# Page copies held until the fourth product, nine weight slots instead of eight, expert loops of three items

## The chip, the cores and the metric

The kernel runs on one core of a Trainium2 chip. The metric is the device time of one execution in microseconds (us). A core has TensorE (matrix products; PE in the profile), VectorE (DVE), ScalarE (ACT), GpSimd (POOL) and SyncE (SP), which here only issues transfers, and 16 DMA engines that move data between HBM and the on-chip memory. SyncE, ScalarE and GpSimd each issue into queues of their own, and a queue's transfers run on all 16 DMA engines.

## The reference

One inference step of a hybrid decoder layer over 256 prompt tokens and 64 sampled ones (8 requests of 8 tokens), all in float32:

```
u = rmsnorm(x)
z = u @ w_in + b_in                       # 1024 -> 6968 columns, feeds both mixers and both gates
h_m = mlstm(z)                            # short convolution, matrix memory
h_n = nsa(z, cache_kv[page_table], ...)   # compressed, selected and window attention
x = x + (g_m * (h_m @ w_bm) + g_n * (h_n @ w_bn)) @ w_out
v = rmsnorm(x)
for each expert e among the top 4 of 32 of a token:
    gu = v @ w_gu[e] + b_gu[e]            # 1024 -> 2048: gate and up
    x += weight * (swiglu(gu) @ w_dn[e] + b_dn[e])
y = rmsnorm(x) * normf_g
```

The past keys and values of the 8 requests lie in 64 pages of a pool, in the order of a page table. Besides `y` the step returns the new keys and values, the convolution rows and the memory states. Each expert has 8 MB of gate and up weights and 4 MB of down weights, and all 32 are read: 403 MB.

## The kernel before, in words

The work of each engine is written out by hand; engines meet at semaphores, and each engine and each issuing queue goes through its own list in order.

The front (`front`) normalises the tokens and multiplies them with `w_in`, which SyncE loads in column chunks of 2 MB into two slots (L122, in `load_chunk`). Chunks 0 and 1 give eight products with the weights held still (L382; each ends with a step of the semaphore `s_pd`); a chunk's slot is free after its four products, and SyncE then loads the chunk after the next one: the third chunk waits for `s_pd` 4, the fourth for `s_pd` 8. The third to sixth chunks give token products in four groups of three (L401, L405), each group from one chunk. Beside this, GpSimd makes constants and masks and then copies the 64 cache pages into one linear tensor in HBM, `kv_linear` (L290), each copy behind a small load of the page's number. After the copies stand, on GpSimd's list, the stores of the convolution rows and the memory states. Attention over the prompt and over the samples follows the front.

The last part (`tail`) merges the branches (L1983), multiplies with `w_out` (L1994, L2003), routes tokens to experts and runs the experts. Work comes as items: an item is up to 64 tokens of one expert, at least one item for each of the 32 experts. The weights of an item are six chunks of 2 MB (four of gate and up, two of down), each in a slot of a ring of `NSLOT` tiles. Chunk n of the whole stream goes to slot `SLOT_ORDER[n % NSLOT]`. Six of the slots are tiles of their own, which first hold the branch weights (slots 0 to 3) and `w_out` (4 and 5); the others lie in the big tile `zf`, whose earlier contents are dead by then. SyncE issues the first `NSLOT` chunks as these become free: the first four after pairs of branch products (`s_pe`), two after the gating of the branches (`s_ev`), the rest after the output projection (`s_po`). From then on chunk n waits for the use of the chunk that had its slot, counted by `s_used` (L1716, in `load_chunk_of`).

TensorE does an item in two functions: `gate_up` (L2133, one use of a chunk after each two of eight steps, with the scatter of the item before in the middle) and `down` (L2174), which first gathers and transposes the next item's tokens. Because slots must be known when the program is built, the loop over items has a body of four items (`QUADS` turns of it; 4 x 6 chunks are three rounds of eight slots), and the items after that, up to a count known only on the chip, run in a loop of one item that always uses the same six slots. Two loads of items stand ahead of the loop on SyncE. The small buffers of an item (`xe`, `atT`, `y3`, `oh`, `up`, `sg` and others) lie in the upper part of `zf`. The gain of the final norm, repeated over the partitions (`gf`, three loads), is loaded by SyncE ahead of the first expert chunk.

Of the kernel before, what the change touches and what calls it, by code (L numbers as in the profile page):

```python
# [45 lines left out]
NE = 32  # L46
FE = 1024
SLOT = 64
N_OVER = 20
NITEM = NE + N_OVER  # L50
NCHUNK = 6
NSLOT = 8
SLOT_ORDER = (0, 1, 2, 3, 6, 7, 4, 5)

# [70 lines left out]
def front(nc, m, a):  # L125
# [59 lines left out]
    with ExitStack() as c:  # L185
# [51 lines left out]
        def _(pool):  # L237
# [47 lines left out]

            pool.wait_ge(s_pages, 16)
            for b in range(NB):
                for j in range(NPG):
                    page = pool.value_load(m.pages[0:1, b * NPG + j:b * NPG + j + 1], min_val=0, max_val=a.cache_kv.shape[0] - 1)
                    pool.dma_start(m.kv_lin[b, j], a.cache_kv[bass.ds(page, 1)].rearrange("n r l c g d -> r (n l c g d)")).then_inc(s_lin, 16)  # L290
# [1417 lines left out]
def load_chunk_of(sp, m, a, e, c, slot):  # L1708

    if c < 4:  # L1710
        src = a.w_gu[0, bass.ds(e, 1), c * 256:(c + 1) * 256, :].rearrange("e (p j) n -> p (e j) n", p=128)
        dst = m.ring[slot][:, :].rearrange("p (j n) -> p j n", j=2)
    else:
        src = a.w_dn[0, bass.ds(e, 1), (c - 4) * 512:(c - 3) * 512, :].rearrange("e (p j) n -> p (e j) n", p=128)
        dst = m.ring[slot][:, :].rearrange("p (j n) -> p j n", j=4)
    sp.dma_start(dst, src).then_inc(m.s_slot[slot], 16)  # L1716


def load_gain(sp, tile, gain, sem):

    sp.dma_start(tile[:, 0:2, :].rearrange("p h n -> p (h n)"), gain.to_broadcast((128, D))).then_inc(sem, 16)
    for h in range(2):
        sp.dma_start(tile[h * 64:(h + 1) * 64, 2, :], gain[:, h * H:(h + 1) * H].to_broadcast((64, H))).then_inc(sem, 16)


def tail(nc, m, a):
# [27 lines left out]
    s_oh, s_ohe, s_gat, s_xg = sem("ex_onehot"), sem("ex_onehot_e"), sem("ex_gathered"), sem("ex_x")  # L1754
    s_xh, s_xr, s_xm, s_xl = sem("xn2_high"), sem("xn2_rest"), sem("xn2_middle"), sem("xn2_low")
    s_yh, s_yr, s_ym, s_ohz = sem("ex_y_high"), sem("ex_y_rest"), sem("ex_y_middle"), sem("ex_onehot_dup")
# [7 lines left out]
    PER = 4  # L1764
    QUADS = 7
    SCATTER_BANKS = (6, 7, 4, 5, 0)
# [5 lines left out]
    flat_zf = m.zf[:, :, :].rearrange("p k n -> p (k n)")  # L1772
    m.ring += [flat_zf[:, 0:4096], flat_zf[:, 4096:8192]]
    at_word = 8192

    def carve(n):
        nonlocal at_word
        at_word += n
        return flat_zf[:, at_word - n:at_word]

    def halves(words, parts):
        return words.bitcast(BF).rearrange("p (t s) -> p t s", t=parts)

    WORDS = PARTS * H // 2
    xT = flat_zf[:, 8192:10240].rearrange("p (k n) -> p k n", k=KD)
    xe, atT = (carve(4 * 2 * SLOT).rearrange("p (k h s) -> p k h s", k=4, h=2) for _ in range(2))
    y3 = halves(carve(3 * H // 2), 3)
    oh = carve(NT * SLOT).rearrange("p (t s) -> p t s", t=NT)
    ohe = carve(SLOT)[0:3 * NE, 0:SLOT // 2].bitcast(BF)
    assert at_word == 10240  # L1790
    xg, gt, up, sg, y_rest = (carve(H) for _ in range(5))
    xT2 = gt.rearrange("p (k n) -> p k n", k=4)
    with ExitStack() as c:
        def sb(name, shape, dt=FP):
            return c.enter_context(nc.sbuf_tensor(name, shape, dt))

        x = sb("x", [128, PARTS, H])
        xn = sb("xn2", [128, PARTS, H])
        g2, gf = sb("g2b", [128, 3, H]), sb("gf", [128, 3, H])
        g2c, br, wr = sb("g2c", [128, KD]), sb("brb", [128, NE]), sb("w_r", [128, KD, NE])  # L1800
        t1 = xn[:, 0, 0:NTOK]
        words = lambda t: t[:, :, :].rearrange("p t s -> p (t s)")
        x_rest, g2w = words(xn), words(g2)
        b_rest = x_rest[0:3 * NE, H:H + 2 * FE]
        xs_high, xs_mid = halves(m.masks[:, 0:WORDS], PARTS), halves(g2w[:, 0:WORDS], PARTS)
        xs_low = [halves(g2w[:, WORDS:WORDS + H // 2], 1), halves(x_rest[:, 0:H], 2), halves(x_rest[:, H:2 * H], 2)]
# [23 lines left out]
        sel, sel_b = sb("sel", [128, NT, NE]), sb("sel_b", [128, 2, NE], BF)  # L1830
        posT = sb("posT", [NE, NT * 128])
        cnt, ext, cse, cs = (sb(n, [NE, 1]) for n in ("cnt", "ext", "cse", "cs"))
# [5 lines left out]
        own = of_expert[0:NE, NE:NITEM]  # L1838
        bdn = sb("bdn", [SLOT + NE, H])
        wtT2 = sb("wtT", [SLOT + NE, NT * 128])  # L1840
# [11 lines left out]
        def slot_of(i, ch):  # L1852
            return SLOT_ORDER[(NCHUNK * i + ch) % NSLOT]

        def round_of(i, ch):
            return (NCHUNK * i + ch) // NSLOT

        @block.sync
        def _(sp):
# [16 lines left out]
            sp.dma_start(br[:, :], a.b_router.to_broadcast((128, NE))).then_inc(s_g, 16)  # L1876
            load_gain(sp, gf, a.normf_g.rearrange("(o n) -> o n", o=1), s_gf)
            for n in range(NSLOT):
# [7 lines left out]
            for n in range(NSLOT, 2 * NCHUNK):  # L1886
                sp.wait_ge(s_used, n + 1 - NSLOT)
                load_chunk_of(sp, m, a, 1, n - NCHUNK, slot_of(1, n - NCHUNK))
            with sp.Fori(0, QUADS) as q:
                for j in range(2, 6):  # L1890
                    for ch in range(NCHUNK):
                        sp.wait_ge(s_used, 4 * NCHUNK * q + (NCHUNK * j + ch + 1 - NSLOT))
                        load_chunk_of(sp, m, a, 4 * q + j, ch, slot_of(j, ch))
            sp.wait_ge(s_tab, 1)
            nw = n_items(sp)
            with sp.Fori(4 * QUADS + 2, nw) as i:
                e = sp.value_load(etab[0:1, bass.ds(i, 1)], min_val=0, max_val=NE - 1)

                for ch in range(NCHUNK):
                    sp.wait_ge(s_used, NCHUNK * i + (ch + 1 - NCHUNK))  # L1900
                    load_chunk_of(sp, m, a, e, ch, slot_of(1, ch))
# [15 lines left out]
        def _(pe):  # L1917
# [277 lines left out]
            nw = n_items(pe)  # L2195
            pe.wait_ge(s_xl, 1)
            down(1, first_slot, lambda ch: 16)
            with pe.Fori(0, QUADS) as q:
                for j in range(1, 5):
                    slot = lambda ch: slot_of(j, ch)  # L2200
                    loaded = lambda ch: 16 * 3 * q + 16 * (round_of(j, ch) + 1)
                    gate_up(4 * q + j, slot, loaded)
                    down(4 * q + (j + 1), slot, loaded)
            later = 4 * QUADS + 1
            slot = lambda ch: slot_of(later, ch)
# [9 lines left out]
        def _(act):  # L2215
# [52 lines left out]
            act.wait_ge(s_wtT, 1)  # L2268
            copy(posT[:, :], m.bank[0][0:NE, 0:NT * 128], s_wTe)
            act.wait_ge(s_wtT, 2)  # L2270
# [4 lines left out]
            copy(words(xs_high), x_rest, s_xh)  # L2275
            act.wait_ge(s_xr, 1)
            copy(words(xs_mid), x_rest, s_xm)
            act.wait_ge(s_own, 1)
# [39 lines left out]
        def _(dve):  # L2318
# [194 lines left out]
            dve.wait_ge(s_xh, 1)  # L2513
            dve.tensor_tensor(x_rest, x_rest, words(xs_high), ALU.subtract).then_inc(s_xr, 1)
            add_bias()
            dve.wait_ge(s_xm, 1)
            for low, r, n in zip(xs_low, (0, 1, 3), (1, 2, 2)):
# [193 lines left out]
```

## Time and profile before

| | us |
|---|---|
| median of three runs (lowest, highest) | 1600.58 (1599.12, 1600.83) |
| the profiled execution | 1597.34 |
| its span (first to last recorded work) | 1595.7 |
| TensorE busy, share of the span | 1513.4, 95% |
| VectorE busy, share | 546.0, 34% |
| ScalarE busy, share | 316.4, 20% |

The page gives each engine's busy time, the span in 40 equal slices (here 39.9 us each), the DMA queues, the chain of work that ended last, the costliest groups of instructions and the DMA issues. Times in the views count from the start of the span. A group is a line of the kernel, an engine, an operation and its operands; "idle before" is what the engine waited just before it, and the arrow names what ended that wait. In views of one row for several instructions the first number is the start of the first and the second the time to the end of the last. The granted clock of TensorE is a share of 2.4 GHz.

### The profile page before, as it was taken

Reading aid. Unit: us, or ns where it says so; the run is one execution under the profiler, and the core shown is the slowest. Engines: PE = TensorE matmul, PEld = TensorE weight load, DVE = VectorE, ACT = ScalarE, POOL = GpSimd, SP = SyncE. Lnnn points to the kernel's source line nnn. Section 1 sums busy time; section 2 is a strip of 40 time slices with the busy share of each in tenths; the row PEclk is TensorE's granted clock in tenths of the full one; section 3 lists DMA queues with packets and bytes.
Section 4 is the critical chain, followed back from the end, with each engine's and each line's share of the span. In section 5 each row is a group of like instructions: output and inputs, shape, how many; then the busy total and the mean of one; then the engine's idle time right before and its main releaser. Section 6 shows DMA issues by size and latency. Waiting matters only on the chain.

```text
span 1595.7 us, 22043 instructions
## 1 busy us (share of the span) xinstructions
PE 1513.4 (95%) x8565; PEld 712.0 (45%) x8565; DVE 546.0 (34%) x1184; ACT 316.4 (20%) x711; POOL 53.5 (3%) x121
## 2 busy tenths in 40 slices
PE   8999998999989999999999999999999999999996
PEld 5547554666766675333333333333333333333332
DVE  4511333244457432623323232232322322322323
ACT  2301221234236400311111111111111111111112
POOL 5410000000000000000000000000000000000000
PEclk9999998799999999999999999999999999999998
DMA  9933356134464396699999999999999999999995
GB/s 344 390 126 106 119 185 133 54 106 182 146 172 160 92 304 284 238 374 427 428 428 427 428 428 428 428 427 427 428 428 428 428 427 428 428 428 428 426 427 225
DMA packets 99712, 507.33 MB, mean 318 GB/s; under 512 B 19126, under 2 KB 57386, under 8 KB 73896
## 3 DMA queue, kind: packets, MB, share of 16 engines
q1 hardware_dynamic: 95522, 482.78, 76.2%
q0 software_dynamic: 4080, 23.73, 4.0%
q8 instruction: 38, 0.62, 0.2%
q14 instruction: 18, 0.15, 0.0%
q10 hardware_dynamic: 54, 0.05, 0.0%
HBM read 499.38 MB, written 28.06 MB: 331 GB/s over the span
## 4 chain that ended last, share of the span: by engine, by line
PE 32%; DMA 30%; DVE 3%; issue 1%; SPq 0%; ACT 0%; DVEq 0%
DMA wring<-w_gu 25%; PE bank L2133 14%; PE bank L2174 8%; DMA zf<-w_gu 4%; PE bank L1983 3%; PE bank L1994 2%; PE bank L2075 1%; PE bank L1966 1%; DVE zf L2504 1%; DVE zf L2506 1%; DVE zf L2502 1%; DMA wring<-w_branch_n 1%; PE bank L2003 0%; PE bank L1962 0%; PE bank L2108 0%
## 5 line engine op out<-in xcount | busy, mean ns | idle before, releaser
L2133 PE MATMUL bank<-wring,zf 128*64 128x512 f32 x1600 | 360.4, 596 | 25.0 <-DMA wring<-w_gu 24.7
L2133 PEld LDWEIGHTS bank<-wring,zf 128*64 128x64 f32 x1600 | 108.7, 136 | 250.3 <-issue 192.4
L2486 DVE SCALAR_TENSOR_TENSOR x<-bank,wt,x 128x512 f32<-128x512 f32 x155 | 104.9, 744 | 196.3 <-PE bank L2075 196.3
L2174 PE MATMUL bank<-wring,zf 128*64 128x512 f32 x768 | 170.1, 595 | 0.7
L2217 ACT ACTIVATE zf<-bank 128x512 f32<-128x512 f32 (+1 forms) x133 | 75.8, 594 | 316.1 <-PE bank L2174 214.8
L2133 PE MATMUL bank<-zf 128*64 128x512 f32 x448 | 100.8, 596 | 6.2 <-DMA zf<-w_gu 6.2
L2492 DVE TENSOR_TENSOR zf<-bank,zf 128x512 f32<-128x512 f32 x32 | 22.1, 692 | 224.6 <-ACT zf L2217 224.6
L2174 PEld LDWEIGHTS bank<-wring,zf 128*64 128x64 f32 x768 | 53.4, 137 | 98.9 <-issue 96.9
L954 PE MATMUL bank<-uT,w_slots 128*128 128x320 f32 x256 | 81.1, 465 | 1.2 <-ACT zf L1087 1.2
L2075 PE MATMUL bank<-zf,eqw 64*128 64x512 bf16 x558 | 69.3, 380 | 0.0
L1983 PE MATMUL bank<-zf,wring 128*128 128x320 f32 x240 | 65.1, 433 | 1.6 <-DMA wring<-w_branch_n 1.3
L2217 ACT ACTIVATE eqw<-bank 128x320 bf16<-128x320 f32 x32 | 14.0, 438 | 259.4 <-PE bank L2075 259.4
L2133 PEld LDWEIGHTS bank<-zf 128*64 128x64 f32 x448 | 31.2, 136 | 68.7 <-issue 54.9
L2499 DVE TENSOR_SCALAR zf<-bank 128x512 f32<-128x512 f32 x32 | 22.1, 692 | 112.8 <-PE bank L2133 112.6
L954 PEld LDWEIGHTS bank<-uT,w_slots 128*128 128x128 f32 x256 | 49.7, 204 | 22.7 <-issue 5.8
L2284 ACT ACTIVATE zf<-zf 128x512 f32<-128x512 f32 x32 | 20.1, 629 | 192.3 <-DVEq L2500 192.3
L2174 PE MATMUL bank<-zf 128*64 128x512 f32 x256 | 56.7, 595 | 0.0
L1983 PEld LDWEIGHTS bank<-zf,wring 128*128 128x128 f32 x240 | 45.4, 190 | 21.3 <-DMA wring<-w_branch_n 1.8
L401 PE MATMUL bank<-w_slots,uT 128*128 128x512 f32 (+1 forms) x128 | 52.1, 566 | 2.4 <-DMA w_slots<-w_in 2.4
L2075 PEld LDWEIGHTS bank<-zf,eqw 64*128 64x128 bf16 x558 | 23.3, 98 | 56.3 <-issue 38.3
L1966 PE MATMUL bank<-ident,zf 128*128 128x128 f32 x260 | 35.9, 280 | 11.6 <-DVEq L2507 11.3
L2102 PE MATMUL bank<-g2b,eqw 128*64 128x512 bf16 (+1 forms) x224 | 44.3, 385 | 0.0
(530 smaller groups left out, 1699.3 us busy)
## 6 DMA issues: line engine op xcount, KB each, us to landing
wring<-w_gu SPq DMA_DIRECT2D x100, 2048.0 KB, 32.6
wring<-w_dn SPq DMA_DIRECT2D x48, 2048.0 KB, 34.5
zf<-w_gu SPq DMA_DIRECT2D x28, 2048.0 KB, 32.8
zf<-w_dn SPq DMA_DIRECT2D x16, 2048.0 KB, 34.3
w_slots<-w_in SPq DMA_DIRECT2D x11, 2048.0 KB, 8.7
kv_linear<-cache_kv POOLq DMA_DIRECT2D x64, 256.0 KB, 5.3
kv_stage<-kv_linear SPq DMA_DIRECT2D x16, 1024.0 KB, 9.2
w_slots<-w_in SPq DMA_DIRECT2D x4, 1024.0 KB, 7.8
```

The lines of the kernel that those rows point to most:

```text
L401: last = pe.matmul(m.bank[n % 4][:, 0:width], uT[:, k, t * 128:(t + 1) * 128], w[:, s, k, 0:width], start=(k == 0), stop=(k == KD - 1))
L954: last = pe.matmul(m.bank[7][:, 0:NTOK], m.w_slots[:, chunk % NSL, k, j % 4 * 128:(j % 4 + 1) * 128], m.uT[:, k, :], start=(k == 0), stop= ...
L1966: last = pe.transpose(m.bank[bank][:, k * 128:(k + 1) * 128], src[:, k * 128:(k + 1) * 128], m.ident[:, :])
L1983: last = pe.matmul(m.bank[2 * i + f % 2][:, 0:NTOK], wb[:, i, k, f % 2 * 128:(f % 2 + 1) * 128], h[:, k, :], start=(k == 0), stop=(k == KD ...
L1994: last = pe.matmul(m.bank[4 + 2 * t + h][:, :], mT[:, k, t * 128:(t + 1) * 128], w_out(k, h), start=(k == 0), stop=(k == KD - 1))
L2075: last = pe.matmul(out, ohtb[rows, t * 128:t * 128 + TILE_ROWS[t]], y3[rows, q, :], start=(q == 0), stop=(q == 2))
L2102: last = pe.matmul(half(0, h), oh2[rows, t, 0:SLOT], x_part(q, 2 * t + h if t < 2 else 4)[rows, :], start=(t == 0 and q == 0), stop=(t == ...
L2133: last = pe.matmul(half(2 + gu, h), xe[:, k % 4, k // 4, :], m.ring[slot(k // 2)][:, o:o + H], start=False, stop=(k == KD - 1))
L2174: last = pe.matmul(half(4, h), atT[:, k % 4, k // 4, :], m.ring[slot(4 + k // 4)][:, o:o + H], start=(k == 0), stop=(k == 7))
L2217: act.activation(dst, src, ACT.Copy).then_inc(to, 1)
L2486: dve.scalar_tensor_tensor(part(r), m.bank[SCATTER_BANKS[r]][:, :], wt[:, r // 2, bass.ds(i - 1, 1)], part(r), ALU.mult, ALU.add).then_inc ...
L2492: dve.tensor_tensor(y_rest, m.bank[4][:, :], y3[:, 0, :], ALU.subtract).then_inc(s_yr, 1)
```

## The change

Three edits are made together.

1. GpSimd waits for the fourth product (`s_pd` 4) before the first page copy.
2. The ring has nine slots. The ninth is the part of `zf` where the item's buffers lay. These buffers move into a tile of their own (`item_work`, `item_x`) and into tiles that are dead by then (`xn2`, `bdn`, the tile of the transposed logits). The final gain has no tile any more: it is loaded into slot 3 of the ring, which the last items do not use, after its last chunk was used. Two pairs of semaphores become one each, with two counts.
3. The loops have a body of three items and nine turns (3 x 6 chunks are two rounds of nine slots), so the loop of one item starts at item 28 for TensorE (29 before) and at load 29 for SyncE (30 before).

```diff
-NSLOT = 8
-SLOT_ORDER = (0, 1, 2, 3, 6, 7, 4, 5)
+NSLOT = 9
+SLOT_ORDER = (0, 1, 2, 3, 6, 7, 4, 5, 8)
...
             pool.wait_ge(s_pages, 16)
+            pool.wait_ge(s_pd, 4)
             for b in range(NB):
...
-    QUADS = 7
+    TRIPLES = 9
...
-    m.ring += [flat_zf[:, 0:4096], flat_zf[:, 4096:8192]]
+    m.ring += [flat_zf[:, 0:4096], flat_zf[:, 4096:8192], flat_zf[:, 8192:12288]]
...
-    xg, gt, up, sg, y_rest = (carve(H) for _ in range(5))
+    gt = flat_zf[:, 12288:12288 + H]
...
-        g2, gf = sb("g2b", [128, 3, H]), sb("gf", [128, 3, H])
+        g2, work = sb("g2b", [128, 3, H]), sb("item_work", [128, 3 * H])
+        gf = m.ring[3][:, 0:3 * H].rearrange("p (h n) -> p h n", h=3)
+        xe, y3 = by_half(work[:, 0:H]), halves(work[:, H:H + 3 * H // 2], 3)
...
+        xg = sb("item_x", [128, H])[:, :]
...
+        up, sg, y_rest = (x_rest[:, (2 + i) * H:(3 + i) * H] for i in range(3))
...
-        bdn = sb("bdn", [SLOT + NE, H])
+        bdn_words = sb("bdn", [128, H])
+        bdn, atT = bdn_words[0:SLOT + NE, :], by_half(bdn_words[:, :])
...
-            load_gain(sp, gf, a.normf_g.rearrange("(o n) -> o n", o=1), s_gf)
             for n in range(NSLOT):
...
-            with sp.Fori(0, QUADS) as q:
-                for j in range(2, 6):
+            with sp.Fori(0, TRIPLES) as q:
+                for j in range(2, 5):
                     for ch in range(NCHUNK):
-                        sp.wait_ge(s_used, 4 * NCHUNK * q + (NCHUNK * j + ch + 1 - NSLOT))
-                        load_chunk_of(sp, m, a, 4 * q + j, ch, slot_of(j, ch))
+                        sp.wait_ge(s_used, 3 * NCHUNK * q + (NCHUNK * j + ch + 1 - NSLOT))
+                        load_chunk_of(sp, m, a, 3 * q + j, ch, slot_of(j, ch))
+            sp.wait_ge(s_used, NCHUNK * 3 * TRIPLES + 4)
+            load_gain(sp, gf, a.normf_g.rearrange("(o n) -> o n", o=1), s_gf)
             sp.wait_ge(s_tab, 1)
             nw = n_items(sp)
-            with sp.Fori(4 * QUADS + 2, nw) as i:
+            with sp.Fori(3 * TRIPLES + 2, nw) as i:
...
-            with pe.Fori(0, QUADS) as q:
-                for j in range(1, 5):
+            with pe.Fori(0, TRIPLES) as q:
+                for j in range(1, 4):
```

On GpSimd, at the first page copy after the masks, the list reads before as follows (the semaphore `s_pages` is `pages_in`, `s_pd` is `mx_done`):

```order
L247 AFFINE_SELECT seq_onehot<-seq_onehot 64x8
L289 TENSOR_LOAD pages [waits pages_in]
L289 ISA x2
L290 ISA
L290 DMA kv_linear<-cache_kv 16x4096
```

and with the change:

```order
L247 AFFINE_SELECT seq_onehot<-seq_onehot 64x8
L290 TENSOR_LOAD pages [waits mx_done,pages_in]
L290 ISA x2
L291 ISA
L291 DMA kv_linear<-cache_kv 16x4096
```

Nothing changes its place there; the first load of a page number has a second wait, and the 64 copies and all that follows stand behind it.

On SyncE, where the last part's loads end and the expert chunks begin, the list before (`wring` 0 to 5 are slots 0 to 5, `zf` the slots behind them):

```order
L1876 DMA brb<-b_router 128x32
L1721 DMA gf<-normf_g 128x1024
L1723 DMA gf<-normf_g 64x512 x2
L1716 DMA wring0<-w_gu 128x4096
L1716 DMA wring1<-w_gu 128x4096
L1716 DMA wring2<-w_gu 128x4096
L1716 DMA wring3<-w_gu 128x4096
L1716 DMA zf<-w_dn 128x4096 x2
L1716 DMA wring4<-w_gu 128x4096
L1716 DMA wring5<-w_gu 128x4096
L1716 DMA wring0<-w_gu 128x4096
L1716 DMA wring1<-w_gu 128x4096
```

and with the change, from the second chunk on:

```order
L1717 DMA wring1<-w_gu 128x4096
L1717 DMA wring2<-w_gu 128x4096
L1717 DMA wring3<-w_gu 128x4096
L1717 DMA zf<-w_dn 128x4096 x2
L1717 DMA wring4<-w_gu 128x4096
L1717 DMA wring5<-w_gu 128x4096
L1717 DMA zf<-w_gu 128x4096
L1717 DMA wring0<-w_gu 128x4096
L1717 DMA wring1<-w_dn 128x4096
L1717 DMA wring2<-w_dn 128x4096
```

The three loads of `gf` are gone from this place, and a chunk into `zf` stands before the first chunk that waits for a use. Behind the loop over three items the list on SyncE now has:

```order
L1887 COMPARE_AND_BRANCH
L1722 DMA wring3<-normf_g 128x1024
L1724 DMA wring3<-normf_g 64x512 x2
L1846 TENSOR_LOAD etab
L1846 ISA x2
L1896 UNCONDITIONAL_BRANCH
```

The loads of the gain stand between the two loops, ahead of the load of the item count (`etab`).

## Rows read from the trace of the kernel before

**Rows 1.** The page's second part: clock and traffic in 40 slices of 39.9 us.
```profile
PEclk9999998799999999999999999999999999999998
...
GB/s 344 390 126 106 119 185 133 54 106 182 146 172 160 92 304 284 238 374 427 428 428 427 428 428 428 428 427 427 428 428 428 428 427 428 428 428 428 426 427 225
```

**Rows 2.** The chain in order of time: start us, us, what.
```profile
719.85 6.87 PE bank L2133 x32
...
938.72 6.87 PE bank L2133 x32
...
1030.11 35.35 DMA wring<-w_gu
...
1118.36 35.34 DMA wring<-w_gu
...
1565.65 3.68 PE bank L2133 x16
```

**Rows 3.** TensorE's timeline, 60 to 105: start us, us, line, operation [idle before].
```profile
63.85 15.70 PE L401 MATMUL bank<-w_slots,uT 128*128 128x512 f32 x32 [2.38 <-DMA w_slots<-w_in]
...
83.97 13.90 PE L401 MATMUL bank<-w_slots,uT 128*128 128x512 f32 x32
...
101.41 14.00 PE L401 MATMUL bank<-w_slots,uT 128*128 128x512 f32 x32
```

**Rows 4.** Windows of 1 us: busy by engine, granted clock, DMA share, GB/s.
```profile
62.00:63.00 1.00, 0.00 (x0) 0.00 (x0) 0.87 (x1) 0.59 (x3) 0.21 (x1) 1.00 0.99 375
66.00:67.00 1.00, 1.00 (x2) 0.34 (x1) 0.06 (x2) 0.98 (x2) 0.49 (x1) 0.50 1.12 442
```

**Rows 5.** Windows over the start of the weight stream, columns as in rows 4.
```profile
590.00:596.00 6.00, 6.00 (x24) 4.21 (x23) 3.43 (x4) 0.00 (x0) 0.00 (x0) 1.00 1.08 324
626.00:649.00 23.00, 22.75 (x115) 9.46 (x113) 8.55 (x32) 3.37 (x10) 0.00 (x0) 1.00 0.01 2
651.40:686.20 34.80, 33.28 (x195) 14.02 (x195) 21.06 (x57) 13.54 (x19) 0.00 (x0) 0.95 0.88 354
686.20:690.20 4.00, 4.00 (x22) 1.31 (x20) 0.00 (x0) 0.00 (x0) 0.00 (x0) 1.00 0.26 53
691.00:985.00 294.00, 289.71 (x1584) 104.88 (x1581) 91.79 (x162) 42.66 (x75) 0.00 (x0) 1.00 1.01 427
```

**Rows 6.** SyncE's timeline, 640 to 700: expert chunks issued.
```profile
649.33 18.55 SPq L1716 DMA_DIRECT2D wring<-w_gu  x4
674.06 3.76 SPq L1716 DMA_DIRECT2D wring<-w_dn  x2
688.85 3.75 SPq L1716 DMA_DIRECT2D zf<-w_gu  x2
```

**Rows 7.** GpSimd's timeline: the first and the last of 64 page copies.
```profile
12.52 0.72 POOL L290 DMA_DIRECT2D kv_linear<-cache_kv  x1 [0.68 <-issue]
...
84.01 0.49 POOL L290 DMA_DIRECT2D kv_linear<-cache_kv  x1 [0.63 <-issue]
```

**Rows 8.** Line 122 alone: loads of w_in, issue (duration, start) and landing.
```profile
L122 SPq DMA_DIRECT2D w_slots<-w_in x1: 2313/2313/2313, 39.9 to 39.9; - x1
...
DMA to landing us min/median/max: 23.9/23.9/23.9
...
L122 SPq DMA_DIRECT2D w_slots<-w_in x1: 367/367/367, 57.1 to 57.1; - x1
...
DMA to landing us min/median/max: 19.6/19.6/19.6
...
L122 SPq DMA_DIRECT2D w_slots<-w_in x1: 367/367/367, 83.2 to 83.2; - x1
...
DMA to landing us min/median/max: 13.3/13.3/13.3
```

**Rows 9.** DMA issues of the final gain: count, KB each, median us to landing.
```profile
gf<-normf_g SPq DMA_DIRECT2D x1, 512.0 KB, 14.3
...
gf<-normf_g SPq DMA_DIRECT2D x2, 128.0 KB, 14.5
```

More of the change, by code:

```diff
@@ L1754, in tail @@
     s_oh, s_ohe, s_gat, s_xg = sem("ex_onehot"), sem("ex_onehot_e"), sem("ex_gathered"), sem("ex_x")
-    s_xh, s_xr, s_xm, s_xl = sem("xn2_high"), sem("xn2_rest"), sem("xn2_middle"), sem("xn2_low")
+    s_xh, s_xl = sem("xn2_high_then_middle"), sem("xn2_rest_then_low")
     s_yh, s_yr, s_ym, s_ohz = sem("ex_y_high"), sem("ex_y_rest"), sem("ex_y_middle"), sem("ex_onehot_dup")
@@ L1772, in tail @@
     flat_zf = m.zf[:, :, :].rearrange("p k n -> p (k n)")
-    m.ring += [flat_zf[:, 0:4096], flat_zf[:, 4096:8192]]
[L1774 to L1779, printed above, removed]
+    m.ring += [flat_zf[:, 0:4096], flat_zf[:, 4096:8192], flat_zf[:, 8192:12288]]
     def halves(words, parts):
@@ L1785, in tail @@
     xT = flat_zf[:, 8192:10240].rearrange("p (k n) -> p k n", k=KD)
[L1786 to L1790, printed above, removed]
-    xg, gt, up, sg, y_rest = (carve(H) for _ in range(5))
+    gt = flat_zf[:, 12288:12288 + H]
     xT2 = gt.rearrange("p (k n) -> p k n", k=4)
@@ L1798, in tail @@
         xn = sb("xn2", [128, PARTS, H])
-        g2, gf = sb("g2b", [128, 3, H]), sb("gf", [128, 3, H])
+        g2, work = sb("g2b", [128, 3, H]), sb("item_work", [128, 3 * H])
+        gf = m.ring[3][:, 0:3 * H].rearrange("p (h n) -> p h n", h=3)
+        by_half = lambda t: t.rearrange("p (k h s) -> p k h s", k=4, h=2)
+        xe, y3 = by_half(work[:, 0:H]), halves(work[:, H:H + 3 * H // 2], 3)
+        at_word = H + 3 * H // 2
+        oh = work[:, at_word:at_word + NT * SLOT].rearrange("p (t s) -> p t s", t=NT)
+        ohe = work[0:3 * NE, at_word + NT * SLOT:at_word + NT * SLOT + SLOT // 2].bitcast(BF)
+        xg = sb("item_x", [128, H])[:, :]
         g2c, br, wr = sb("g2c", [128, KD]), sb("brb", [128, NE]), sb("w_r", [128, KD, NE])
@@ L1830, in tail @@
         sel, sel_b = sb("sel", [128, NT, NE]), sb("sel_b", [128, 2, NE], BF)
-        posT = sb("posT", [NE, NT * 128])
+        posT = words(pl)[0:NE, :]
         cnt, ext, cse, cs = (sb(n, [NE, 1]) for n in ("cnt", "ext", "cse", "cs"))
@@ L2195, in _ @@
             nw = n_items(pe)
-            pe.wait_ge(s_xl, 1)
+            pe.wait_ge(s_xl, 2)
             down(1, first_slot, lambda ch: 16)
-            with pe.Fori(0, QUADS) as q:
-                for j in range(1, 5):
+            with pe.Fori(0, TRIPLES) as q:
+                for j in range(1, 4):
                     slot = lambda ch: slot_of(j, ch)
[L2201 to L2204, printed above, removed]
+                    loaded = lambda ch: 16 * 2 * q + 16 * (round_of(j, ch) + 1)
+                    gate_up(3 * q + j, slot, loaded)
+                    down(3 * q + (j + 1), slot, loaded)
+            later = 3 * TRIPLES + 1
             slot = lambda ch: slot_of(later, ch)
@@ L2268, in _ @@
             act.wait_ge(s_wtT, 1)
-            copy(posT[:, :], m.bank[0][0:NE, 0:NT * 128], s_wTe)
+            copy(posT, m.bank[0][0:NE, 0:NT * 128], s_wTe)
             act.wait_ge(s_wtT, 2)
@@ L2275, in _ @@
             copy(words(xs_high), x_rest, s_xh)
-            act.wait_ge(s_xr, 1)
-            copy(words(xs_mid), x_rest, s_xm)
+            act.wait_ge(s_xl, 1)
+            copy(words(xs_mid), x_rest, s_xh)
             act.wait_ge(s_own, 1)
@@ L2513, in _ @@
             dve.wait_ge(s_xh, 1)
-            dve.tensor_tensor(x_rest, x_rest, words(xs_high), ALU.subtract).then_inc(s_xr, 1)
+            dve.tensor_tensor(x_rest, x_rest, words(xs_high), ALU.subtract).then_inc(s_xl, 1)
             add_bias()
-            dve.wait_ge(s_xm, 1)
+            dve.wait_ge(s_xh, 2)
             for low, r, n in zip(xs_low, (0, 1, 3), (1, 2, 2)):
```

## The prediction

> **What bounds the kernel now.** I read four views, in this order.
>
> First, the page's second part, for the traffic in each of 40 slices. The last half of the span, from about 720 us, moves 426 to 428 GB/s in every slice but the last [rows 1]. The expert weights come in chunks of 2048 KB, that is 2.097 MB, six to an item. A chunk therefore takes 2.097 MB / 428 GB/s = 4.90 us of the queue.
>
> Second, the chain of waits in order of time. Up to about 985 us it runs through TensorE: the product of item 2 starts at 719.85 and that of item 10 at 938.72, so an item costs (938.72 - 719.85) / 8 = 27.36 us there [rows 2]. Later the same place in the chain waits for a chunk: 1030.11 and 1118.36 are three items apart, so an item costs 29.42 us, which is six times 4.90. TensorE is faster than the weights, has caught up with them by then, and from there the end of the weight stream sets the end of the kernel: the last gate product starts at 1565.65, as its chunk lands, and about 30 us of work follow. So anything that starts the stream earlier, or takes bytes out of it, shows in full at the end. A few us of TensorE time inside an expert item do not.
>
> Third, TensorE's timeline of the first 130 us. It is busy without a gap but for one place: the first token product (L401) starts at 63.85 after 2.38 us of waiting for a chunk of w_in [rows 3]. TensorE does nothing in 62 to 63, and the granted clock is 0.50, its 1.2 GHz level, in 66 to 67 [rows 4]. The 32 records of that product take 15.70 us; the same 32 records later take 13.90 [rows 3]. Lost at this place: 2.38 + 1.80 = 4.18 us. Time lost here moves everything behind it, the start of the weight stream too, since that start hangs on products.
>
> Fourth, SyncE's timeline and the windows over the stage where the stream starts. The queue has two holes there. From 626 to 649 it moves 2 GB/s [rows 5]: all free slots are filled and two wait for the output projection. The issues that follow go out at 649.33, 674.06 and 688.85 [rows 6]. From 686.2 to 690.2 the queue moves 53 GB/s, and from 691 on it is full again, at 427 [rows 5].
>
> **The change, part by part.**
>
> Page copies. GpSimd issues 64 copies from 12.52 to 84.01, one in each (84.01 - 12.52) / 63 = 1.13 us [rows 7]. SyncE issues the third chunk of w_in at 39.9, and it lands 23.9 us later, at 63.8 [rows 8]: that is the wait of TensorE. SyncE's issue and the new wait of GpSimd release on the same event, the fourth product. So the copies move to about 40 to 112 us. Before 40, 24 copies of 256 KB (6.3 MB) leave the queue. The state loads that stood ahead of the chunk then land before it is issued. What is left is the chunk beside the copies. The nearest row for that: chunk four, issued at 57.1, lands at 76.7, and its forerunner landed at 63.8, so a chunk beside copies costs 12.9 us, and with some 2 us to the first byte about 15. From 39.9 this gives 55, and TensorE wants it at 61.5. The bounds are the fastest landing here, 13.3 us, and the 19.6 of chunk four, which still shared with its forerunner; both are under 21.6. The wait of 2.38 goes. I let the slow clock go with it, since nothing else stops TensorE there: -4.18 us, with bounds of -2.38 and -4.18.
>
> What is queued behind the new wait on GpSimd: the small stores of convolution rows and of the state's maxima, which go out some 27 us later, and the state stores of the heads, which wait for much later products. Nobody reads any of these, and the copied pages are first read after the front is over. The chunks to be loaded after it now share with copies. The tightest is chunk five: issued at 83.2 and wanted at 101.41, it has 18.2 us [rows 3, 8]. Both ends move with TensorE, so at 15 us it costs nothing. It is priced as a rival.
>
> In the Trainium skill, "DMA: Bandwidth & Descriptors" (Queues, rings and completion order) says that each DMA engine goes round between the queues that have work for it, a packet at a time. By that rule the chunk would get half of some 400 GB/s and take an estimated 10.5 us; rows 8 show 12.9, so the copies took more than half. By the rule chunk five has more room than by the row, and the sum is the same by both.
>
> Ninth slot. Before, eight chunks go out by 649.33 and a bit, and chunk n later waits for use n - 7. After, a ninth goes out right behind the two at 649.33, and each later chunk waits for one use fewer. TensorE's uses do not move. So the issue that ends at 667.9 (649.33 + 18.55), the two of 674.06 and that of 688.85 each carry the chunk after the one they carry now. The hole of 686 to 690 stays, but 13 chunks instead of 12 are through before it. There is room for that: from 651.4 to 686.2 the queue moves 354 GB/s, or 5.9 chunks, where 428 would be 7.1 [rows 5]. After the hole the queue is full in both, so the rest of the stream is one chunk shorter: -4.90 us. Bounds: 0, if the chunk found no idle time, and -4.90, since the rest cannot be shorter by more than a chunk. I take -4.90, the end that the idle time of the row allows.
>
> The same page of the Trainium skill (Where 436 GB/s comes from) says that for loads into the on-chip memory the HBM side binds, at about 358 GB/s a core. By it the chunk would be worth an estimated 5.9 us. This trace shows 428, and the row decides.
>
> Final gain (gf). Its three loads, 512 + 2 x 128 KB or 0.786 MB [rows 9], leave their place ahead of the first expert chunk and come back inside the full stream, behind chunk 173 (counted from 0). Taking them out early saves nothing: they and the first six chunks are through by 626, and the idle 23 us behind that take up any gain. Coming back they lengthen the stream. At 428 GB/s that is 1.84 us. But the stretch in which such repeated rows went before, 590 to 596, moved only 324 GB/s [rows 5], which makes 2.43. If all that is missing there against 428, 1.46 us, were theirs, it is 3.30. Bounds 1.84 and 3.30; I take 2.43, from the row nearest to it.
>
> Loops over three items, shared tiles. Two turns of four end between the two items from which 27.36 us came, and in the second half TensorE waits for chunks anyway. The last three items instead of two run on six slots. There five chunks, 24.5 us of queue, are ahead of TensorE, which lets at most 11 us pass between two uses (677.8 to 688.85 in rows 6). The traffic in the slices with six slots is 428 before [rows 1]. I count 0. The new tiles stand where the old ones were read and written in the same order on the same engines: 0. Two semaphores became counts on others, with the same events: 0.
>
> Sum: -4.18 - 4.90 + 2.43 = -6.65 us on the profiled execution's 1597.34, which gives 1590.69. The three runs have a median of 1600.58, 3.24 above the profiled one, which I add unchanged: 1593.9.
>
> **The rivals.**
>
> A, the clock falls all the same. For it: the page's clock row is below full in two slices, from 239 to 319 us, with no load on its chain [rows 1]. Against it: in rows 4 it is 1.00 right before this wait. The front is then worth 2.38: -4.85, 1595.7.
>
> B, the slot does not do what it says: the stream gains a chunk at the start and loses one again, because three items on six slots, with a new load between the two loops, let the queue run dry once. For it: the issues stop for two uses where nine slots become six. Against it: the same step from eight to six is in the profile, at full rate. Then -4.18 + 2.43 = -1.75: 1598.8.
>
> C, slower. The copies, now held until 112 us, collide with chunk five. Its place is the product at 101.41 and its slack 18.2 us. At 19.6 us, as chunk four had, TensorE waits 1.4 and pays 1.8 for the clock: 1597.1. At 23.9, as chunk three had, it waits 5.7 + 1.8 = 7.5, more than the 6.65 gained: 1601.4. It decides from a landing of 23.1 us on. For it: 13.3 us for chunk five already now, with only two copies still to be issued. Against it: in the 23.9 were 2 MB of state ahead of the chunk, which are gone by then.
>
> **How the numbers follow.** The forecast 0.62, A 0.17, B 0.11, C 0.10. Against no change, a measurement of this kernel can tell about 0.2%, here 3.2 us, so faster is below 1597.4. The forecast and most of A lie there, and of C the part near 19.6: 0.82. B, the upper edge of A and the middle of C are the same: 0.13. C past 26 us, and what I may have missed, is slower: 0.05. The range: at the low end all terms at their best are -7.24, 1593.3, and the shown runs with the profiled one differ by 3.5 us, so 1590.8. At the high end A and the lower half of C are inside, B mostly not: 1597.8.
>
> **What the profile after would show.** TensorE without a wait before its first token product, that product in 13.9 us at granted clock 1.00, and copies issued from about 40 to 112. A third issue right behind the two after the output projection; the hole in the queue still there, about 4 us earlier; the first wait of a product for an expert chunk two to three items later than now. The three gf loads some 140 us before the end, and the stream a chunk less 2.4 us shorter from the hole to its end. A wait of the third group of token products (C), or a stretch below 420 GB/s late in the stream (B), would make it wrong.

## The result, and the profile after

The changed kernel takes 1586.83 us (median of seven runs, 1585.56 to 1593.64) where the kernel before takes 1598.66 (seven runs, 1595.69 to 1600.83): a ratio of 0.9939, 95% interval 0.9921 to 0.9957. The forecast was 1593.9, and its range ended at 1590.8. The sign was right, the gain was larger than forecast.

| profiled execution | before | after |
|---|---|---|
| its time, us | 1597.34 | 1586.25 |
| span, us | 1595.7 | 1584.6 |
| mean granted clock | .985 | .989 |
| last down product starts, us | 1573.07 | 1562.04 |

The page's second part, clock and traffic in 40 slices of 39.6 us, answers to [rows 1]:

```profile
PEclk9999998899999999999999999999999999999998
...
GB/s 248 316 313 96 135 171 134 55 153 137 147 173 161 117 327 221 322 394 427 427 429 426 428 429 426 428 429 426 428 428 427 429 426 428 429 426 427 414 428 221
```

Traffic has left the first slice, where the copies were. One slice near the end, the 38th, has fallen to 414: the final gain is in it.

TensorE's timeline of the first 130 us answers to [rows 3] (start us, us, line, operation, and in brackets the idle time before, if any):

```profile
62.04 14.00 PE L402 MATMUL bank<-w_slots,uT 128*128 128x512 f32 x32
...
80.47 13.90 PE L402 MATMUL bank<-w_slots,uT 128*128 128x512 f32 x32
...
97.90 14.00 PE L402 MATMUL bank<-w_slots,uT 128*128 128x512 f32 x32
```

There is no bracket at the first line, and its 32 records take 14.00 us, not 15.70: the wait is gone, and the slow clock with it. The 14.00 was also the right length to compare with; the prediction took the 13.90 of the later product. The windows of [rows 4] now show a busy TensorE at full clock:

```profile
62.00:63.00 1.00, 1.00 (x4) 0.49 (x3) 0.99 (x1) 0.83 (x2) 0.37 (x2) 1.00 1.20 487
66.00:67.00 1.00, 1.00 (x4) 0.51 (x3) 0.70 (x3) 0.99 (x2) 0.49 (x1) 1.00 1.02 416
```

GpSimd's timeline shows the hold, in answer to [rows 7]:

```profile
42.12 0.72 POOL L291 DMA_DIRECT2D kv_linear<-cache_kv  x1 [30.74 <-issue]
...
113.71 0.49 POOL L291 DMA_DIRECT2D kv_linear<-cache_kv  x1 [0.63 <-issue]
```

The loads of w_in, each by itself, answer to [rows 8]:

```profile
DMA to landing us min/median/max: 10.7/10.7/10.7
...
L122 SPq DMA_DIRECT2D w_slots<-w_in x1: 368/368/368, 79.7 to 79.7; - x1
...
DMA to landing us min/median/max: 16.5/16.5/16.5
```

The third chunk lands 10.7 us after its issue (before: 23.9). Chunk five, of the second pair, is issued at 79.7, lands at 96.2 and is wanted at 97.90.

SyncE's timeline shows the ninth slot, in answer to [rows 6]:

```profile
641.65 0.80 SPq L1717 DMA_DIRECT2D wring<-w_gu  x2
642.50 0.43 SPq L1717 DMA_DIRECT2D zf<-w_gu  x1
655.29 0.33 SPq L1717 DMA_DIRECT2D wring<-w_gu  x1
659.88 6.83 SPq L1717 DMA_DIRECT2D wring<-w_dn  x2
```

The third issue of 642.50 is the new one. The windows (length, busy time of the five engines, granted clock, DMA share, GB/s) answer to [rows 5], and the last two show what is new:

```profile
644.00:678.20 34.20, 32.69 (x199) 13.78 (x199) 20.80 (x57) 13.55 (x19) 0.00 (x0) 1.00 0.99 419
678.20:682.00 3.80, 3.80 (x20) 1.29 (x18) 0.00 (x0) 0.00 (x0) 0.00 (x0) 1.00 0.50 108
683.00:1050.00 367.00, 362.19 (x1977) 130.45 (x1973) 114.08 (x202) 53.22 (x94) 0.00 (x0) 1.00 1.01 428
1470.00:1475.00 5.00, 4.99 (x29) 1.91 (x29) 0.68 (x3) 1.08 (x2) 0.00 (x0) 1.00 1.03 339
1475.00:1480.00 5.00, 3.16 (x18) 0.94 (x14) 0.90 (x2) 1.23 (x2) 0.00 (x0) 1.00 0.99 405
```

The stretch ahead of the hole is filled, from 354 to 419 GB/s, and the hole is still there. At 1470 to 1480 the gain goes by, at 339 and 405 where 428 is usual.

The chain of waits (start us, us, what) answers to [rows 2]:

```profile
1069.66 40.24 DMA wring<-w_gu
```

This is its first long wait for an expert chunk. Before, the first one stood here:

```profile
993.21 33.02 DMA wring<-w_gu
```

From the start of item 0 (651.60 now, 659.27 then) these are 418.1 and 333.9 us. The difference of 84.1 is three items of 27.4: one chunk of lead keeps TensorE free of the queue for three items longer, as forecast.

### The profile page after: what moved, and what is told of

The parts are those of the page before. It is cut to its first block, busy times and chain, and to the rows that moved or that the text cites. A ratio compares the mean times of both kernels' runs of the same rounds, so it can differ in the third digit from the quotient of the medians.

```text
span 1584.6 us, 22070 instructions
## 1 busy us (share of the span) xinstructions
PE 1506.0 (95%) x8565; PEld 709.2 (45%) x8565; DVE 545.7 (34%) x1184; ACT 316.3 (20%) x711; POOL 53.2 (3%) x121
## 4 chain that ended last, share of the span: by engine, by line
PE 38%; DMA 24%; DVE 4%; issue 1%; SPq 0%; ACT 0%; DVEq 0%
DMA wring<-w_gu 23%; PE bank L2133 17%; PE bank L2174 10%; PE bank L1983 3%; PE bank L2075 2%; PE bank L1994 2%; PE bank L1966 2%; DVE xn L2504 1%; DVE xn L2506 1%; DVE xn L2502 1%; DMA wring<-w_branch_n 1%; PE bank L1962 1%; PE bank L2003 0%; PE bank L2108 0%; PE bank L2061 0%
## 5 line engine op out<-in xcount | busy, mean ns | idle before, releaser
L2133 PE MATMUL bank<-wring,item_work 128*64 128x512 f32 x1552 | 349.6, 595 | 26.4 <-DMA wring<-w_gu 26.1
L2133 PEld LDWEIGHTS bank<-wring,item_work 128*64 128x64 f32 x1552 | 106.9, 136 | 244.3 <-issue 184.6
L2174 PE MATMUL bank<-wring,bdn 128*64 128x512 f32 x560 | 125.0, 596 | 0.1
L2133 PE MATMUL bank<-zf,item_work 128*64 128x512 f32 x496 | 113.0, 597 | 4.6 <-DMA zf<-w_gu 4.6
L2174 PE MATMUL bank<-zf,bdn 128*64 128x512 f32 x464 | 103.3, 594 | 0.1
L2217 ACT ACTIVATE item_work<-bank 128x512 bf16<-128x512 f32 (+1 forms) x65 | 38.6, 595 | 215.3 <-PE bank L2174 214.3
L2174 PEld LDWEIGHTS bank<-wring,bdn 128*64 128x64 f32 x560 | 38.1, 137 | 70.1 <-issue 67.6
L2075 PE MATMUL bank<-item_work,eqw 64*128 64x512 bf16 x558 | 69.2, 380 | 0.0
L2133 PEld LDWEIGHTS bank<-zf,item_work 128*64 128x64 f32 x496 | 33.3, 136 | 73.2 <-issue 64.7
L2174 PEld LDWEIGHTS bank<-zf,bdn 128*64 128x64 f32 x464 | 32.3, 137 | 61.8 <-issue 60.7
## 6 DMA issues: line engine op xcount, KB each, us to landing
w_slots<-w_in SPq DMA_DIRECT2D x11, 2048.0 KB, 10.7
```

What stands on the lines that cost most here:

```text
L2075: last = pe.matmul(out, ohtb[rows, t * 128:t * 128 + TILE_ROWS[t]], y3[rows, q, :], start=(q == 0), stop=(q == 2))
L2133: last = pe.matmul(half(2 + gu, h), xe[:, k % 4, k // 4, :], m.ring[slot(k // 2)][:, o:o + H], start=False, stop=(k == KD - 1))
L2174: last = pe.matmul(half(4, h), atT[:, k % 4, k // 4, :], m.ring[slot(4 + k // 4)][:, o:o + H], start=(k == 0), stop=(k == 7))
L2217: act.activation(dst, src, ACT.Copy).then_inc(to, 1)
```

## The experiments

The profiled pair differs by 11.03 us at the last down product. From the starts of the same products in both TensorE timelines, -3.50 stand at the end of the first token product, and -3.36 behind the first product of the output projection. Another -4.25 lie between 80 and 416 us, in stages that the change does not touch. They go with the clock: TensorE has 0.76 in one 70 us window there before, 0.83 after, and 0.07 of 70 us is an estimated 4.9 us of work at full clock.

```profile
250.00:320.00 70.00, 64.05 (x373) 41.69 (x367) 21.45 (x45) 13.25 (x39) 0.75 (x2) 0.76 0.44 91
```

```profile
245.00:315.00 70.00, 64.39 (x403) 42.16 (x400) 23.90 (x50) 15.25 (x42) 1.09 (x2) 0.83 0.44 94
```

Of the -3.36, 1.6 is clock as well: from the output projection to the first down product the profile before takes 75.55 us (clock 0.98) and the one after 73.96 (clock 1.00), and a second profile of the kernel before takes 73.96 too.

Theory 1 said that this clock is luck, and that the change itself is worth what was forecast. Theory 2 said that the change lifts the clock there. The first four kernels shared a chip and 31 runs of the kernel before, with a median of 1596.67 us (1591.14 to 1603.26).

**The kernel before once more.**

> The kernel before once more, for the spread of its executions. Theory 1 (luck of the clock): the time at half clock, 2 x (1 - mean granted clock) x span, differs between executions of one and the same kernel, and the time follows it with some 0.4 us per us; the mean clock goes over a range like the 0.983 to 0.989 of the changed kernel, so some executions here have 0.987 or more and then take about 1594 us. Theory 2 (the change lifts the clock): all executions lie at or below 0.986, where the changed kernel has 0.989 in most.

Measured: 1598.05 us, ratio 1.0014 (0.9996 to 1.0031). Ten of its twelve executions have a mean clock of 0.987 or more, where theory 2 allowed 0.986 at most, and its profiled execution has 0.83 in the window of 250 to 320, where the first had 0.76. The clock there changes without any edit, and theory 2 falls. Its first token product shows something else:

```profile
65.61 14.00 PE L401 MATMUL bank<-w_slots,uT 128*128 128x512 f32 x32 [3.01 <-DMA w_slots<-w_in]
```

A wait of 3.01 us, and no slow clock behind it.

**Copies held, nothing else.** The kernel before with the one new wait:

```
             pool.wait_ge(s_pages, 16)
+            pool.wait_ge(s_pd, 4)
```

> The kernel before with the page copies alone held until the fourth product; eight slots as before. Both theories: no wait before the first token product and full clock there, the second token product starts 3.5 us earlier. Theory 1: that is all, 3.5 to 4.2 us faster than before at the median, and more only in executions with a higher mean clock than before. Theory 2: the later places at half clock, 250 to 320 us, shorten too in most executions, 7 to 8 us faster.

Measured: 1590.48 us, ratio 0.9963 (0.9947 to 0.9978); its median is 6.2 below that of the shared runs. The median lies above theory 1's 3.5 to 4.2 and below theory 2's 7 to 8, but the interval, 3.5 to 8.5 us, covers both, so the time alone decides nothing here. Its profile has no wait and 14.00 us for the product.

**Slots without the hold.** The changed kernel without that wait:

```
             pool.wait_ge(s_pages, 16)
-            pool.wait_ge(s_pd, 4)
```

> The changed kernel without the hold of the page copies: nine slots, loops of three items and the gain at the end alone. Both theories: the 2.4 us wait before the first token product is there as before. Theory 1: 4.9 us less for the slot, 3.1 us more for the gain (what the 339 GB/s stretch of the trace after makes of it), so 1.8 us faster, up to 3.4 if the half-clock stretch at 680 us falls away too. Theory 2: the same 1.8 to 3.4, and the rest of the 9.7 with the copies alone.

Measured: 1595.9 us, ratio 0.9999 (0.9981 to 1.0017). By the time alone the slots and the gain are worth between -3.0 and +2.7 us, an inconclusive result. Both theories expected the 2.4 us wait as before. Its profile has, at the same place and with the same code, nearly three times that, and this was the clue to the rest.

```profile
69.14 15.97 PE L401 MATMUL bank<-w_slots,uT 128*128 128x512 f32 x32 [6.71 <-DMA w_slots<-w_in]
```

**The changed kernel once more.**

> The changed kernel once more beside the others on the same chip. Both theories: about 9.7 us below before at the median. Theory 1: compared at equal mean clock the gap to before is 5 to 6.5 us, as the sum of the prediction had it; Theory 2: executions of both kernels hardly share a mean clock at all.

Measured: 1589.08 us, ratio 0.9947 (0.9928 to 0.9965). That is 7.6 below the shared runs, not 9.7. Both kernels have runs at mean clocks of 0.986 to 0.989, which speaks against theory 2 again; at each of these clocks they lie 9 to 12 us apart, not the 5 to 6.5 of theory 1. The two single edits, -6.2 and -0.8 by their medians, add up to the -7.6 of both within the noise.

Theories 1 and 2 had both taken the wait for a constant 2.38. Theory 3, formed here, says that it differs from execution to execution and is about 4 us in the mean. Four more kernels shared another chip (17 runs of the kernel before, median 1596.27).

**The kernel before twice more**, one profiled execution each (1598.92 and 1601.81 us).

> The kernel before once more, for its wait before the first token product. Theory 3 (the wait differs between executions, about 4 us in the mean, profiled so far as 2.38, 3.01 and 6.71): another value between 2 and 7 us. Rival (it is a constant 2.4 to 3.0, and 6.71 came with the ninth slot): 2.3 to 3.1 us.

```profile
67.29 15.51 PE L401 MATMUL bank<-w_slots,uT 128*128 128x512 f32 x32 [4.72 <-DMA w_slots<-w_in]
```

> The kernel before once more, for the same wait: by theory 3 a value between 2 and 7 us that differs from the other looks by over 1 us in at least one of the two; by the rival 2.3 to 3.1 us in both.

```profile
68.19 17.05 PE L401 MATMUL bank<-w_slots,uT 128*128 128x512 f32 x32 [7.11 <-DMA w_slots<-w_in]
```

These two waits differ from each other by 2.4 us and both lie above the 2.3 to 3.1 of the rival, a constant wait; the second is just past the 7 of theory 3. Five profiled executions of a front without the hold thus show waits of 2.38, 3.01, 4.72, 6.71 and 7.11, mean 4.79. The product behind them exceeds 14.00 by 1.70, 0.00, 1.51, 1.97 and 3.05, mean 1.65. The sum is 6.4 us in the mean, from 3.0 to 10.2, and holding the copies alone measured 6.2. The excess is clock: in the last of these executions it is 0.50 for nearly ten microseconds, of which 3.6 lie still in the wait and 6.2 in the product, which takes 3.05 longer for it.

```profile
64.60:74.40 9.80, 6.21 (x8) 2.60 (x9) 5.41 (x14) 5.56 (x9) 4.15 (x9) 0.50 1.01 397
```

The cause of the wait is the landing of one load: 23.9, 24.6, 26.3, 28.3 and 28.7 us after its issue. With the hold, in six executions, it is 9.8 to 10.7. The shortest and the longest of the five, issue and landing (the first stands in [rows 8] as well):

```profile
L122 SPq DMA_DIRECT2D w_slots<-w_in x1: 2313/2313/2313, 39.9 to 39.9; - x1
...
DMA to landing us min/median/max: 23.9/23.9/23.9
```

```profile
L122 SPq DMA_DIRECT2D w_slots<-w_in x1: 6099/6099/6099, 39.5 to 39.5; - x1
...
DMA to landing us min/median/max: 28.7/28.7/28.7
```

Most of this difference is there before the chunk is issued. The two loads of state stand just ahead of it on SyncE, and here are their issues in the same two executions:

```profile
L333 SPq DMA_DIRECT2D state_ce<-state_C x2: 3774/3918/4063, 28.5 to 32.6; - x2
```

```profile
L333 SPq DMA_DIRECT2D state_ce<-state_C x2: 3148/3743/4338, 31.7 to 36.1; - x2
```

In the order of the waits, the second state load is issued at 32.6, 34.5, 35.6, 36.1 and 36.1, and the chunk lands 31.2, 31.1, 31.7, 33.0 and 32.1 us after that: a spread of 1.9 us where the landings themselves spread over 4.8. With the hold it is issued at 23.4 to 24.1. The first page copy starts at 12.5 in the two executions with the shortest waits and at 11.5 in the three others, as here:

```profile
11.52 1.01 POOL L290 DMA_DIRECT2D kv_linear<-cache_kv  x1 [0.33 <-issue]
```

Where the copies start earlier, SyncE gets through its list later and the chunk lands later; this was read from five executions and not tested by an edit.

**State loads behind the chunk, copies not held.** What makes the chunk late, the 2 MB of state ahead of it in its own queue or the copies beside it? The kernel before, with

```
-            for h in range(2):
-                sp.dma_start(ce[h]..., a.state_C[0, :, h]...).then_inc(s_c0[h], 16)
             for i in range(NSL, C_BG + 2):
...
                 load_chunk(sp, m, a, i)
+                if i == NSL:
+                    for h in range(2):
+                        sp.dma_start(ce[h]..., a.state_C[0, :, h]...).then_inc(s_c0[h], 16)
```

> The kernel before, page copies not held, but the two state loads of SP (1 MB each) behind the third projection chunk instead of ahead of it. Theory 3a (bytes ahead of the chunk in its own queue make the wait; the copies only slow them down): the chunk lands 18 to 20 us after its issue, TensorE does not wait before the first token product, and the time falls as with the held copies, 5 to 6 us, ratio 0.996 to 0.997, with as small a spread (under 2 us). Theory 3b (the copies halve the chunk's rate whatever lies ahead): it lands after 22 to 27 us, the wait of 2 to 7 us stays, ratio 0.999 to 1.001, spread 3.5 us as before.

Measured: 1598.49 us, ratio 1.001 (0.9992 to 1.0028). TensorE's timeline:

```profile
62.04 14.00 PE L402 MATMUL bank<-w_slots,uT 128*128 128x512 f32 x32
...
84.02 15.58 PE L402 MATMUL bank<-w_slots,uT 128*128 128x512 f32 x32 [3.39 <-DMA w_slots<-w_in]
```

The third chunk lands after 15.9 us (3a said 18 to 20) and the first wait is gone, as 3a said; but the time has not fallen by the 5 to 6 us of 3a, and its runs spread as before. The fourth chunk, now behind the state, takes 26.2 and TensorE waits 3.39 one product later, with the same slow clock (15.58 for 13.90). Theory 3b had the landing wrong and the time right. Beside copies that are under way the third chunk thus takes 15.9 us with the state behind it and 23.9 to 28.7 with the state ahead of it; where the state has landed before and the copies start just behind the chunk, it takes about 10. So state and copies together are too much for the queues before 84 us, and moving the state only moves the wait. What helps is to send the copies later.

**The gain at the end of the queue.** The changed kernel, with load_gain issued behind the last item's chunks. The tile that it fills is not used by the last loop.

```
-            sp.wait_ge(s_used, NCHUNK * 3 * TRIPLES + 4)
-            load_gain(sp, gf, ..., s_gf)
             sp.wait_ge(s_tab, 1)
...
                     load_chunk_of(sp, m, a, e, ch, slot_of(1, ch))
+            sp.wait_ge(s_used, NCHUNK * 3 * TRIPLES + 4)
+            load_gain(sp, gf, ..., s_gf)
```

> The changed kernel with one thing moved: the final norm's gain (0.786 MB in three loads) is issued behind the last item's chunks, not in the full stream. Theory 3 (gain costs what its bytes and its slow movement take out of a full queue): the stretch 1470:1480 us moves at 428 GB/s again and the last product ends about 3.1 us earlier than in the changed kernel (2.43 by the prediction's term, 1.84 by bytes alone); time about 1585.6 us where the changed kernel has 1588.7, ratio to before about 0.9925; the gain lands some 5 us before the final norm reads it. Rival (the stream has slack there, the gain is hidden): no difference from the changed kernel, ratio 0.994 to 0.995. Rival (the gain becomes the last arrival at the end): 1 to 3 us slower than the changed kernel, with VectorE waiting for the gain's load.

Measured: 1586.16 us (six runs), ratio 0.9937 (0.9915 to 0.9958). This interval takes in both the 0.9925 of theory 3, which here says that the gain costs the full queue some 3 us, and the 0.994 to 0.995 of the rival that it costs nothing; the traces decide. The windows where the gain was:

```profile
1470.00:1475.00 5.00, 4.63 (x37) 2.38 (x35) 2.94 (x7) 1.68 (x3) 0.00 (x0) 1.00 0.99 419
1475.00:1480.00 5.00, 5.00 (x26) 1.62 (x24) 0.00 (x0) 0.00 (x0) 0.00 (x0) 1.00 1.03 436
```

The chain gives the length of the stream's part, from the first down product to the last, here and then in the changed kernel:

```profile
679.03 7.02 PE bank L2174 x32
...
1562.25 7.11 PE bank L2174 x32
```

```profile
675.79 7.02 PE bank L2174 x32
...
1562.04 7.11 PE bank L2174 x32
```

883.22 against 886.25: the gain costs 3.03 us inside the stream and none at its end, where it lands about 1566 and is first read by VectorE at 1577.20 (issued at 1540.64 and just behind; KB each and us to landing):

```profile
wring<-normf_g SPq DMA_DIRECT2D x1, 512.0 KB, 24.2
wring<-normf_g SPq DMA_DIRECT2D x2, 128.0 KB, 25.2
```

**Both side by side, on the second chip.**

> The version with the final gain at the end of the queue once more, beside the changed kernel on the same chip. Theory 3 (the gain in the full stream costs 2.4 to 3.1 us): its median lies 2 to 3 us below that of e8_after, about 1586 us, ratio to before 0.992 to 0.9935. Rival (no cost; the first comparison came from different chips): medians within 0.8 us.

Measured: 1586.96 us, ratio 0.9934 (0.9911 to 0.9957); down to down 883.20 us.

> The changed kernel once more, for the comparison with e8_gain_last: 1588 to 1589 us, ratio to before 0.994 to 0.9955; no wait of TensorE for a load before the first token product, by every theory.

Measured: 1587.96 us, ratio 0.9949 (0.9929 to 0.9968); down to down 886.51 us, and no wait at the first token product. In the traces the stream is 3.3 us shorter. In time the two medians lie only 1.0 apart, with six runs each: between the 2 to 3 of theory 3 and the 0.8 of the rival, so these runs alone do not decide. With the earlier runs they are 1586.2 (12 runs) and 1588.7 (23 runs), 2.5 apart. So this has the lowest median of the case, and its traces show why, though its interval overlaps that of the changed kernel.

## Why the prediction was too small

The gap of 7.1 us between 1593.9 and 1586.83 splits in three, with the runs of all chips pooled: before 1597.25 (79 runs), after 1588.68 (23 runs).

- The starting point: 1600.58, the median of the three runs shown, is 3.3 above the median of 79. A third of the kernel's runs lie above 1599, and three drawn at once give no better base. The change was added to it unmodified. This is the largest share.
- The change: forecast -6.65, pooled -8.6. This is the error of the argument, 1.9 us.
- The changed kernel's first seven runs lie 1.85 below its 23, which is luck.

The range was narrow by a slip as well: 1593.3 less the 3.5 by which the runs differ is 1589.8, not 1590.8, and still above the measured time.

Term by term:

**Page copies, forecast -4.18. Beside the starting point, this is the step that failed, in size.** The mechanism holds: the hold takes the wait and the slow clock away, and no product of TensorE waits for what stands behind it on GpSimd. But "lost at this place: 2.38 + 1.80" read the price from one execution, and of five that was the shortest wait. Its upper bound in the prediction, -4.18, was no bound: three of the five executions lost 6.2 to 10.2 us, the mean of all five is 6.4, and holding the copies alone measured 6.2 (3.5 to 8.5). The row that could have warned stood in [rows 8]: a landing of 23.9 us where another chunk took 13.3 in the same trace is a load that others can push about. The chunk's landing after the change, put at about 15, is 10.7, and chunks four and five take 16.5 each. From the Trainium skill, "DMA: Bandwidth & Descriptors" (Queues, rings and completion order), whose rule is that a DMA engine takes turns between the queues, the prediction had worked out an estimate of 10.5. The trace agrees for the third chunk and not for the two after it.

**Ninth slot, forecast -4.90.** Right. From the first down product to the last, the chain has 887.97 us with the hold alone:

```profile
675.93 7.02 PE bank L2175 x32
...
1563.90 7.11 PE bank L2175 x32
```

With the ninth slot and the gain at the end it has 883.22, that is -4.75, one chunk. All six profiles with eight slots have 887.97 to 888.41, and both with the gain at the end 883.20 and 883.22: -4.9 in the mean. The issues, the fuller stretch, the hole (8 us earlier than before and not 4, with the clock's share of the front) and the three items of later waits came as forecast.

**Final gain, forecast +2.43, bounds 1.84 and 3.30.** 3.03 and 3.31 in the pairs above (886.25 and 886.51 against 883.22 and 883.20), and by the other two profiles with nine slots and the gain inside (886.75 and 886.86) 3.5 and 3.7; 2.5 in the pooled medians. So it was priced too low, by 0.6 to 1.2 us in the traces, and the upper bound was about the middle of what came. The prediction took the middle row; the bound that gave the whole shortfall to these loads was closer.

**Loops and tiles, forecast 0.** Nothing in the traces speaks against it: the queue moves 428 GB/s through the six-slot stretch once the gain is out.

With -6.4, -4.9 and +3.4 the sum is -7.9, beside -8.6 measured by the pooled medians. The remaining 0.7 us is not explained; since the 6.4 is a mean of five values from 3.0 to 10.2, it is no more than the noise. At equal mean clock (0.988, by straight lines through 72 and 23 runs) the two kernels lie 9.5 apart, so up to 1.6 us may have no term here.

**The rivals.** A did not happen where the wait was: no profile of a kernel with the hold shows a low clock in 62 to 75. It was right in that the later low clock, in 250 to 320, stayed: 0.78 to 0.83 in six profiles with the hold, 0.76 to 0.88 in five without. B did not happen: no stretch runs dry. C did not happen, but closely: in six profiles with the hold chunk five lands 13.0 to 17.8 us after its issue, against the 18.2 of slack. The cover held by 0.4 us in the worst of them (80.2 + 17.8 against a product at 98.41).

One reading was loose: TensorE's first 130 us have waits of 5.88 and 1.35 us at their start too, which the change does not touch.

What stays open: why the copies start, and SyncE gets through its list, at different times in executions of the same program; whether that order of events is the cause of the late landing, which no edit tested; and whether chunk five is ever late in runs without a profile.

## What to carry to other kernels

A wait for a load that lands beside other traffic is a draw, not a constant. One profile gives one draw; profile several executions of the unchanged kernel before pricing its removal, and take the base time from many runs for the same reason. Where a queue is full to the end, a small load belongs behind the last large one, if what it feeds starts late enough: there it cost nothing, and inside the stream it cost 3.0 to 3.7 us for 0.79 MB.

## What the runs showed of the hardware

- One 2 MB load behind 2 MB of state and beside page copies landed between 23.9 and 28.7 us after its issue over five executions; with the state behind it, in one execution, 15.9; with the first copy issued after it, between 9.8 and 10.7 over six.
- The clock behind a wait is not a fixed price either: the product behind it took no longer after 3.01 us of idle TensorE, 1.70 us longer after 2.38, 3.05 after 7.11.
- Loads that repeat one row over the partitions cost more than their bytes: 0.786 MB at 428 GB/s would be 1.84 us, and the stream lost 3.0 to 3.7.
- Kernels without the hold spread more than those with it at the same mean granted clock: 1.7 us of standard deviation around a straight line of time over clock for the kernel before, 1.4 and 1.8 for the two others without the hold, 0.5 to 0.8 for the three with it. This fits a wait that varies in runs without a profile too.
